# Encoder layer with a two-way expert part: later column loads and earlier row sums at one hand-over

## The reference, cut to what matters

```
q = (x @ w_query).reshape(C, 8, 2, 128)
s = einsum('chpd,hpkd->chpk', q, sub_keys)
sv, si = top_k(s, 16)                      # per head and half
cand = sv[:, :, 0, :, None] + sv[:, :, 1, None, :]
top_s, pos = top_k(cand, 16)               # 16 experts per head
idx = ids of pos; gate = softmax(top_s)    # 8 heads x 16 = 128 experts per token
a = einsum('cd,chkd->chk', x, expert_u[idx])
y = einsum('chk,chkd->cd', gelu(a) * gate, expert_v[idx])
```

## Time and profile before

| | us |
|---|---|
| median of 3 runs | 2799.38 |
| lowest, highest | 2798.16, 2804.54 |
| the profiled execution | 2804.54 |
| its span | 2802.7 |
| PE busy | 2592.5 (92%) |
| DVE busy | 2087.0 (74%) |
| POOL busy | 1592.2 (57%) |
| ACT busy | 537.8 (19%) |

### The profile page before, as it was taken

The page is one execution under the profiler, slowest core; times in us unless marked ns, Lnnn a source line. Parts: engine busy times, 40 slices in busy tenths (PEclk is TensorE's granted clock), DMA queues, the critical chain, the costliest instruction groups (busy, mean ns, idle before and its releaser), DMA issues.

```text
span 2802.7 us, 30907 instructions
## 1 busy us (share of the span) xinstructions
PE 2592.5 (92%) x9957; PEld 1543.6 (55%) x9957; DVE 2087.0 (74%) x4622; ACT 537.8 (19%) x1206; POOL 1592.2 (57%) x1284
## 2 busy tenths in 40 slices
PE   7999989989798998997799899899999999999998
PEld 6867867774234475554544454455544445444454
DVE  1232978889628877899799979977778777877785
ACT  2141151211027015554500000100000000000001
POOL 0000165457766766443288777776866667766671
PEclk9999999999899999998999999999999999999999
DMA  7538789989898998999899999999999999999994
GB/s 243 184 116 307 277 311 407 398 322 323 334 407 273 361 389 303 357 364 341 268 404 406 401 393 411 371 414 414 413 412 413 413 413 413 413 414 414 407 412 180
DMA packets 305988, 996.18 MB, mean 355 GB/s; under 512 B 26432, under 2 KB 107200, under 8 KB 276672
## 3 DMA queue, kind: packets, MB, share of 16 engines
q0 software_dynamic: 184320, 671.17, 62.1%
q1 hardware_dynamic: 69664, 292.02, 26.7%
q10 hardware_dynamic: 51872, 31.46, 3.7%
HBM read 932.68 MB, written 61.87 MB: 355 GB/s over the span
## 4 chain that ended last, share of the span: by engine, by line
PE 34%; DMA 27%; DVE 23%; issue 9%; POOL 4%; ACT 2%; POOLq 0%; DVEq 0%; ACTq 0%
DMA ring<-in_expert_v,idx 15%; PE bank L705 13%; DMA ring<-in_expert_u,idx 10%; DVE ring L1442 7%; PE bank L693 7%; PE o_bank L725 3%; POOL ring L1407 3%; PE bank L991 3%; PE bank L764 3%; PE o_bank L981 2%; DVE h L1442 2%; DVE region_c L1442 2%; DVE neg_max L1536 1%; DVE gate_attn L1795 1%; DVE region_q L1730 1%
## 5 line engine op out<-in xcount | busy, mean ns | idle before, releaser
L1407 POOL DMA_INDIRECT ring<-in_expert_u,idx x468 | 617.4, 1319 | 639.9 <-DVE idx L1746 294.3
L991 PE MATMUL bank<-wslot,gate_attn 128*128 128x512 f32 x1536 | 697.4, 604 | 56.2 <-DVE gate_attn L1795 55.9
L981 PE MATMUL o_bank<-region_a,wslot 128*128 128x384 f32 x2048 | 681.2, 486 | 0.0
L1407 POOL DMA_INDIRECT ring<-in_expert_v,idx x428 | 506.5, 1183 | 300.5 <-issue 118.8
L981 PEld LDWEIGHTS o_bank<-region_a,wslot 128*128 128x128 f32 x2048 | 389.0, 190 | 298.0 <-issue 60.3
L991 PEld LDWEIGHTS bank<-wslot,gate_attn 128*128 128x128 f32 x1536 | 293.8, 193 | 417.9 <-issue 317.0
L1442 DVE CUSTOM_DVE_ANT_0 ring<-ring,h 128x1024 f32<-128x1024 f32 x380 | 451.1, 1221 | 68.2 <-DMA ring<-in_expert_u,idx 65.8
L1459 DVE SCALAR_TENSOR_TENSOR region_b<-ring,dots,region_b 128x1024 f32<-128x1024 f32 x256 | 328.5, 1283 | 120.9 <-DMA ring<-in_expert_v,idx 105.3
L1311 ACT ACTIVATE gate_attn<-o_bank 128x384 f32<-128x384 f32 x128 | 62.9, 491 | 1279.7 <-PE o_bank L981 1279.7
L705 PE MATMUL bank<-region_b,wslot 128*128 128x256 f32 (+1 forms) x768 | 233.3, 462 | 1.6 <-ACT region_b L1028 1.6
L705 PE MATMUL bank<-region_a,wslot 128*128 128x256 f32 (+1 forms) x768 | 226.3, 452 | 1.0 <-ACT region_a L1028 1.0
(11 more groups left out here) (215 smaller groups left out, 2880.7 us busy)
## 6 DMA issues: line engine op xcount, KB each, us to landing
wslot<-in_expert_uT SPq DMA_DIRECT2D x64, 1024.0 KB, 8.1
wslot<-in_expert_v SPq DMA_DIRECT2D x64, 1024.0 KB, 8.0
wslot<-kept_weights SPq DMA_DIRECT2D x53, 1024.0 KB, 8.4
kept_weights<-wslot SPq DMA_DIRECT2D x29, 1024.0 KB, 8.7
expert_weights<-region_p ACTq DMA_DIRECT2D x24, 1024.0 KB, 10.6
wslot<-in_w_in SPq DMA_DIRECT2D x13, 1024.0 KB, 8.0
region_p<-expert_weights SPq DMA_DIRECT2D x8, 1536.0 KB, 12.6
region_s<-expert_weights SPq DMA_DIRECT2D x7, 1536.0 KB, 12.5
```

The source lines that it names most:

```text
L981: ins = nc.tensor.matmul(dense_in[q][:, 0:DENSE_T], u_cols[slot][:, k, :], mergeds[1][:, k, T - DENSE_T:T], start=(k == 0), stop=(k == KD ...
L991: ins = nc.tensor.matmul(dense_out[2 * t + n][:], hidden[q][:, t * P:(t + 1) * P], v_cols[slot][:, n * 512:(n + 1) * 512], start=start, st ...
L1407: nc.gpsimd.indirect_dma_start(ring_row(n), None, expert_u if what == "u" else expert_v, bass.IndirectOffsetOnAxis(ap=ids, axis=0)).then_i ...
```

## The change

Three things change. A constant `COLUMNS_FROM` (65) is new. SP waits ahead of the five loads until PE has filled the bank of job 65, and ahead of the load of columns 2 and 3 until PE has filled that of job 73 (the formula gives 65 for j = 0 and 73 for j = 2). And the last four quads of tile k = 1 are summed behind jobs 64, 66, 68 and 70, where it was 66, 70, 74 and 78. Nothing else moves, and all amounts of work and of bytes stay.

```
+COLUMNS_FROM = 2 * JOBS_PER_TILE + 1
...
-         **{("w", 2 * JOBS_PER_TILE + n): 1 for n in (2, 6, 10, 14)}}))
+         **{("w", 2 * JOBS_PER_TILE + n): 1 for n in (0, 2, 4, 6)}}))
...
             for c in range(HALVES // 2 - WSLOTS, HALVES // 2):
                 filled(sp, *LAST_JOB[LAST_GROUP[1], "query", c])
+            filled(sp, LAST_GROUP[1], "w", COLUMNS_FROM)
             sp.wait_ge(h2t_spilled, 16)
             sp.dma_start(mergeds[1][:, :, T - DENSE_T:T - P], h2t_dram).then_inc(h2t_back, 16)
             for j in range(0, COL_SLOTS, COLS_EACH):
+                filled(sp, LAST_GROUP[1], "w", COLUMNS_FROM + 2 * JOBS_PER_BLOCK * j // COLS_EACH)
                 load_columns(j)
```

## The result

Five timed runs of each: 2799.38 us before (2791.39 to 2807.15), 2818.08 after (2813.60 to 2820.02). The ratio is 1.0062, its 95% interval 1.0043 to 1.0082, so the change costs 12 to 23 us. The forecast was 2813, +13.5 us. The profiled execution after took 2819.67 us, 15.1 more than that of before.

What follows compares the result with a forecast made beforehand. The column stage is bound by DMA bytes, so it shifts with T0, which the starved block 16 store delays: 1368.5 + 18.6 + 19.3 = 1406.4, +13.5 us. Profiled execution 2818.0, median 2813; 8 in 10 range 2797 to 2822.

Steps and rivals of the forecast that it cites:

- T0: DVE's first dot product of the column stage, at 1392.88 us before; forecast at 1406.4, +13.5 us.
- The main step: DMA queues take turns by packet, so block 16's store lands after everything queued beside it, 32.6 us after issue.
- 13.6 MB: Bytes to be sent up to block 16's last packet: five loads, half of quad 31, 12 u rows, the store; 34 us.
- The tail: From block 16's landing to T0: 18.6 us copied from the wait at job 84, plus 19.3 us of DVE jobs.
- the wait at job 84: ACT's 2.77 us wait in the kernel before for a block store; its 18.6 us from move to T0 was copied.
- ACT's one wait: At the move of job 72, one long idle time of 15 to 22 us for block 16's store.
- the step that failed: Ahead of job 71 on PE: quad 31's rows, issued until 1333.3, taken to be there in time for their sum.
- rival three: Quad 31's rows land late, PE stands ahead of job 71; alone +3 to +5 us, part of the 0.17.
- on top of the forecast: PE's wait for quad 31's rows added to the starved store: 2817 us, included in the 0.68.
- Rival two: Faster: block stores get through, u rows are gathered before block 19; T0 -9.7 us, 2790 us; chance 0.12.
- rival one: No measurable change: the stall hides in DVE's existing waits; say 2800 us; 0.17 together with a milder stall.
- the stretch: Time from job 64's start on PE to T0, 68.59 us before; the forecast moved T0 by +13.5 us.

Runs made afterwards that it cites:

- quad31_late: Changed kernel with quad 31 summed behind job 78 instead of job 70: 2816.76 us, one run; from job 64's start to T0 84.14 us.
- before_again: The kernel before, unchanged, run once more as a control: 2806.81 us, one run; from job 64's start to T0 67.43 us.
- The two parts alone: Kernel before with only the early sums, run twice: ratios 1.0011 and 1.0032; with only SP's two waits, run twice: 1.0035 and 1.0042.

## Why the prediction was right

Step by step, times from job 64's start (its own 1324.3 in the forecast, 1320.85 in the profile after):

| step | forecast | measured |
|---|---|---|
| three loads issued | 6.7 | 6.2 |
| block 16's store issued | 11.6 | 10.6 |
| sum of quad 31 ends | 20.4 | 26.3 |
| two loads issued | 24.4 | 31.7 |
| last of the 12 u rows | 24.7 | 30.8 |
| block 16 lands, job 72 moved | 44.2 | 45.4 |
| T0 | 82.1 | 83.1 |

The main step held: everything queued beside block 16 goes first. The store was to take 32.6 us to land and took 34.7. The rate was 409 GB/s for my 400. The bytes were the term that was sized too small: I counted 13.6 MB from q1's first packets on, and there were 0.73 and 0.78 MB from 1330 to 1334 and 13.50 MB from there to 1367, 15.0 in all. 0.64 MB of these are block 17's and stand behind the store, so 14.4 count. The 0.7 MB more are quad 31: I had taken half of it, 1.05 MB, as sent by then, and POOL's queue had moved only 0.33 MB by 1330 from its first gather on.

The tail, from the landing to T0, was taken from one small wait and DVE's pace: 37.9 us forecast, 37.8 measured. That PE starts again at a granted clock of 0.54 and needs 5.48 us for three jobs was in it unspoken, for the wait at job 84 that I copied had the same. PE before, three jobs behind that wait:

```profile
1375.81 5.74 PE L764 MATMUL bank<-consts 128*128 128x128 f32 x24 [3.06 <-issue]
```

ACT's one wait was 14.89 us where I said 15 to 22: just under. I had job 72 ready at 1347, 22.7 us behind job 64; it was ready at 30.5. The reason is the step that failed:

"Quad 31's rows ... I take them to be there in time." They landed 11.5 us behind their issue in the middle and 12.9 for the last, beyond the 9 us from which rival three decides, and PE stood 4.86 us. Slower work on PE behind that came on top: the sum took 3.64 us instead of 1.92, and the two jobs behind it 2.92 instead of 2.05, at a granted clock of 0.58 from 1343.5 to 1350. So rival three happened, with a wait at the upper end of my 3 to 5 us. But its "on top of the forecast" was wrong: the two waits do not add. While PE stood, block 16 was not through, and whoever comes to a store before it lands pays only the time to the landing. `quad31_late` shows that the wait for the store does not need PE's: it was 11.73 us without it. That this wrong step left no mark on the time is luck in the forecast, for I had not said that the store would cover it; had the store landed before job 72 was ready, at 30.5 us, PE's wait would have counted.

The working has one small slip, too. Job 64's sum was to end at 1329.2, and with 1.92 us for job 65 that gives 1331.1 and not 1330.9; the 0.2 us change nothing above.

Rival two falls to the queue counts and to T0; rival one to the ratio, whose interval begins at 1.0043. For the shift of the whole: the stretch grew by 14.55 (by 15.7 against `before_again`) where 13.5 was forecast; the 1 us between is the last line of the table. The forecast for the median, 2813, was 5 us short of the 2818.08. The measured medians differ by 18.7 with an interval of 12 to 23, so 13.5 and 14.55 both lie in it; whether the 4 us above are real, this case doesn't tell. The two parts alone cost more in time than in stretch as well, which may be something small that I have not found, or the choice of the traced execution.

The Trainium skill (DMA: Bandwidth & Descriptors, "Where 436 GB/s comes from") would have put the 13.6 MB at 358 GB/s. The 409 of the window above says again that this limit does not bind here. The Trainium skill (DMA: Bandwidth & Descriptors, "Queues, rings and completion order") says that each DMA engine goes round the queues that have work and takes a whole packet from one before it turns to the next, with some 9 to 17 descriptors to a packet as a rule. The trace agrees with the round: 398 and 398, and 139, 152 and 152, are one for one in the packets that it counts, whatever their size. Whether those are the packets that are meant there, no run here shows.

## What to carry to other kernels

Before transfers are brought together, count packets and not only bytes. Here a store in small pieces landed only when all that was queued beside it had been sent, so ask who waits for such a store. Then either keep the bulk away from it, or make its pieces larger on the side where it is waited for, and count what that does to whoever reads it: here 92 us. Waits that run at the same time don't add, and so a stall that lies inside another one's time is not a second loss. Waits of 3 us for a buffer went away with one more buffer, but only in the kernel in which the stores did not starve.

## What the runs showed that I had not expected

- Issuing a DMA can itself be the wait: ACT's third store behind two of 2048 packets took 10.69 us instead of 0.52, and a second store behind one took 3.91 to 5.30 in three kernels. No idle time is shown for it; it stands in the duration of the `ACTq` row.
- Four gathers of 0.5 MB beside the loads took 11.5 us to land, as the median.
- In the first and the third batch each kernel with early sums had job 67's result reach ACT some 8 us late, put down to "remote"; those of the second batch and the changed kernel did not. Open.
- Two executions of the kernel before had job 64 2.4 us and the stage behind T0 5.9 us apart, so of a change of 15 us the span alone would not have told the place; a distance between two fixed events did.
